# Eight fixed expert weight slots, filled during Wo and the norm, and token stores issued first, in a two-layer decoder step

## What is computed

```python
for layer in range(DEPTH):                       # DEPTH = 2
    if layer < DEPTH_A:                          # layer 0: RWKV-7 time mix
        h, sh, s_fin, v_first = rwkv7_time_mix(x, ...)
    else:                                        # layer 1: dilated window attention
        h = dilated_mixture_attention(x, kv_ext, ...)
    x = layer_norm(ALPHA * x + h, ...)
    m = hier_moe(x, ...)                         # 16 experts, 2 chosen for each token
    x = layer_norm(ALPHA * x + m, ...)
    if layer == DEPTH_A - 1:
        kv_new = einsum('btd,dgsnh->btgsnh', x, p['b_w_kv'])
```

## Time and profile before

| | |
|---|---|
| runs, us | 1735.44, 1732.94, 1730.12; median 1732.94 |
| span of the profiled execution | 1731.9 us (its time from outside is not given; the median of the runs is 1.0 us above the span) |
| busy: TensorE matmul, DVE, ACT, GpSimd | 1557.1, 574.7, 365.6, 196.4 us |
| moved by DMA | 331.28 MB, mean 191 GB/s |
| phases, layer 0 | Wo and norm 482 to 553 us, routing 553 to 578, experts 578 to 861 |
| phases, layer 1 | Wo and norm 1295 to 1366 us, routing 1366 to 1391, experts 1391 to 1673, spill 1675 to 1694 |

### The profile page before, as it was taken

One profiled execution on the slowest core, in us unless ns is written; L12 is line 12 of the kernel. 1 busy time (PEld: TensorE's weight loads), 2 busy tenths in 40 slices (PEclk: granted clock), 3 DMA queues, 4 the chain that ended last, 5 costly groups with the idle time before them and its releaser, 6 DMA issues. The chain is left out here.

```text
span 1731.9 us, 46273 instructions
## 1 busy us (share of the span) xinstructions
PE 1557.1 (90%) x20468; PEld 1156.1 (67%) x20468; DVE 574.7 (33%) x1499; ACT 365.6 (21%) x913; POOL 196.4 (11%) x190
## 2 busy tenths in 40 slices
PE   7999999996897699999859899999999689999980
PEld 6878868875676465555548788887878555555550
DVE  5121445664454321212163100005655521211115
ACT  1023334331501010101131001115650101111113
POOL 1000014643400300000020000000000030000002
PEclk8999999999889799999969999999999789999995
DMA  9410001000523999999971185552120699999994
GB/s 297 164 32 25 1 3 36 29 29 28 181 73 140 339 375 381 383 383 381 373 209 63 64 143 118 126 112 81 44 69 7 229 327 383 380 387 375 385 342 154
DMA packets 218228, 331.28 MB, mean 191 GB/s; under 512 B 70488, under 2 KB 117376, under 8 KB 218032
## 3 DMA queue, kind: packets, MB, share of 16 engines
q1 hardware_dynamic: 193648, 285.33, 48.3%
q0 software_dynamic: 8208, 25.57, 5.5%
q10 hardware_dynamic: 16176, 17.43, 2.9%
HBM read 295.93 MB, written 32.39 MB: 190 GB/s over the span
## 5 line engine op out<-in xcount | busy, mean ns | idle before, releaser
L1979 PE MATMUL bank<-ring_extra,xT 128*32 128x256 f32 x3264 | 181.1, 379 | 0.0
L2443 PE MATMUL bank<-x_early,ring 128*128 128x256 f32 (+1 forms) x768 | 173.5, 387 | 5.7 <-PEq L198 3.9
L1979 PE MATMUL bank<-ring,xT 128*32 128x256 f32 x2880 | 167.3, 388 | 3.2 <-issue 1.6
L2443 PEld LDWEIGHTS bank<-x_early,ring 128*128 128x128 f32 x768 | 146.6, 192 | 28.8 <-issue 4.4
L1979 PEld LDWEIGHTS bank<-ring_extra,xT 128*32 128x32 f32 x3264 | 107.4, 110 | 67.3 <-issue 2.7
L1979 PEld LDWEIGHTS bank<-ring,xT 128*32 128x32 f32 x2880 | 97.6, 112 | 67.1 <-issue 11.6
L1653 DVE TENSOR_TENSOR sg<-sg,bank 128x128 f32<-128x128 f32 x96 | 27.0, 281 | 304.3 <-ACT sg L1832 304.3
L1997 PE MATMUL bank<-ring_extra,hT 128*32 128x256 f32 x1920 | 107.7, 380 | 2.6 <-DVE hT L1661 1.8
L1832 ACT ACTIVATE sg<-bank 128x128 f32<-128x128 f32 x96 | 26.6, 277 | 363.6 <-PE bank L1979 363.6
L376 PE MATMUL bank<-mix,ring 128*128 128x260 f32 x448 | 100.5, 384 | 0.0
L376 PEld LDWEIGHTS bank<-mix,ring 128*128 128x128 f32 x448 | 84.5, 190 | 15.3 <-ACT k L558 2.4
(11 more groups left out here) (416 smaller groups left out, 2309.1 us busy)
## 6 DMA issues: line engine op xcount, KB each, us to landing
ring_extra<-in_moe_w_down SPq DMA_DIRECT2D x40, 1024.0 KB
ring_extra<-in_moe_w_gate SPq DMA_DIRECT2D x70, 512.0 KB, 10.1
ring_extra<-in_moe_w_up SPq DMA_DIRECT2D x70, 512.0 KB, 13.6
ring<-in_moe_w_gate SPq DMA_DIRECT2D x62, 512.0 KB, 6.8
ring<-in_moe_w_up SPq DMA_DIRECT2D x62, 512.0 KB, 13.7
ring<-in_moe_w_down SPq DMA_DIRECT2D x26, 1024.0 KB, 17.4
ring<-in_a_w_rkv SPq DMA_DIRECT2D x12, 1024.0 KB
expert_out<-yo ACTq DMA_DIRECT2D x128, 96.0 KB, 6.4
```

Source lines behind the costliest of these rows:

```text
L1979: ins = pe.matmul(ps[u][32 * q:32 * q + 32, 0:256], xT[:, kt, 32 * u:32 * u + 32], gate_up(w, kt % 2, q), start=kt == 0, stop=kt == KT - 1)
L2443: ins = pe.matmul(ps[2 * (job % 3) + h][:, 0:n], w[:, kt_, rr, :], z[:, kt_, lo:lo + n], start=kt_ == 0, stop=kt_ == 7)
```

## The change

`add_slots` places the eight extra slots at fixed addresses, one call per layer, before `output_norm`. In layer 0 five of them (`dead`) lie where tiles of the time mix are no longer used once its gate is done, and three (`later`) overlap what `output_norm` still reads; in layer 1 all eight lie at the top of the SBUF. `output_norm` gets the range of slots that it may fill, `early_slots`. SP's stream there becomes: load all slots free at the phase's start, store the tokens, then wait for and load the four Wo slots. In `expert_layer` two fences keep the phase's tiles off the slots, a few tiles change places, and the pair gathers and the key/value rows use the six oldest slots (`v_ring`) instead of fixed ones.

```diff
+    def add_slots(self, layer, offsets):
+
+        more = [self.nc.alloc_sbuf_tensor_at(f"ring_extra{layer}{i}", [128, SLOT], F32, offset=at) for i, at in enumerate(offsets)]
+        self.slots = self.slots[0:RING] + [t[:, :] for t in more]
...
-def output_norm(core, z, rows, layer, feed, stop, final_rows, x):
+def output_norm(core, z, rows, layer, feed, stop, final_rows, x, early_slots):
...
             @block.sync
             def _(sp):
-                feed.upto(sp, 4, stop)
+                feed.upto(sp, 0, stop, early_slots)
                 for i, t in enumerate(order):
                     sp.wait_ge(final, i + 1)
                     sp.dma_start(core.tokens[128 * t:128 * t + tile_rows(t), :], final_rows[0:tile_rows(t), t, :]).then_inc(core.tokens_stored, 16)
+                feed.upto(sp, 4, stop, early_slots)
...
-        extra = core.sb(own, "ring_extra", [128, EXTRA, SLOT])
-        core.slots = core.slots[0:RING] + [extra[:, i] for i in range(EXTRA)]
         every = range(RING + EXTRA)
...
-        pair = [extra[:, i].rearrange("p (k d) -> p k d", k=2) for i in range(TILES)]
-        keys_values = [extra[:, i - 1 if i else TILES][:, 0:1536] for i in range(TILES)]
...
         v_ring = [core.slots[s] for s in v_slots]
+        pair = [v_ring[i].rearrange("p (k d) -> p k d", k=2) for i in range(TILES)]
+        keys_values = [v_ring[i - 1 if i else TILES][:, 0:1536] for i in range(TILES)]
...
-                output_norm(core, f["w"], rows, 0, feed, MOE0_END, home, early)
+                rows_end = low + 4 * KT * ROWS + 4 * TILES * D
+                dead = [rows_end + 4 * SLOT * i for i in range(3)] + [low + 5 * 4 * KT * ROWS + 4 * SLOT * i for i in range(2)]
+                later = [low + 4 * 4 * KT * ROWS + 4 * SLOT * i for i in range(2)] + [low + 6 * 4 * KT * ROWS]
+                core.add_slots(0, dead + later)
+                output_norm(core, f["w"], rows, 0, feed, MOE0_END, home, early, range(RING + len(dead)))
...
-            output_norm(core, x, rows, 1, feed, MOE1_END, rows, x)
+            top = SBUF_TOP - 4 * SLOT * EXTRA
+            core.add_slots(1, [top + 4 * SLOT * i for i in range(EXTRA)])
+            output_norm(core, x, rows, 1, feed, MOE1_END, rows, x, range(RING + EXTRA))
```

More of the change, by code:

```diff
@@ L1470, in gate_up, with expert_layer @@
     return slot.rearrange("p (m k n) -> p m k n", m=2, k=2)[:, :, i, 128 * q:128 * q + 128]
-def expert_layer(core, rows, x, layer, stores, feed, stop, next_stop, kv=None):
+def expert_layer(core, rows, x, layer, stores, feed, stop, next_stop, kv=None, fences=None):
     nc, ps, io = core.nc, core.banks, core.io
     with ExitStack() as own:
+        if fences:
+            core.sb(own, "low_fence", [128, fences[0]])
+        v_x = core.sb(own, "spill_x", [128, D])
+        L = core.sb(own, "logits", [128, TILES, 20])
+        g = core.sb(own, "g", [128, TILES, 4, 3])
+        if fences:
+            core.sb(own, "high_fence", [128, fences[1]])
         plan = {"slots": core.sb(own, "slots", [128, 2, TILES], I32), "weights": core.sb(own, "weights", [128, 2, TILES]),
                 "expert": core.sb(own, "expert", [128, SPILLS], I32), "spills": core.sb(own, "spills", [128, 1], I32)}
-        extra = core.sb(own, "ring_extra", [128, EXTRA, SLOT])
-        core.slots = core.slots[0:RING] + [extra[:, i] for i in range(EXTRA)]
         every = range(RING + EXTRA)
         wr, br = core.router[:, layer], core.router_bias[:, layer]
-        L = core.sb(own, "logits", [128, TILES, 20])
-        g = core.sb(own, "g", [128, TILES, 4, 3])
         s = core.sb(own, "s", [128, TILES, 8])
@@ L1509, in expert_layer @@
         yo = [core.sb(own, f"yo{i}", [128, SUBS, 256]) for i in range(2)]
-        v_x, v_y = core.sb(own, "spill_x", [128, D]), core.sb(own, "spill_y", [128, 2, 256])
+        v_y = core.sb(own, "spill_y", [128, 2, 256])
         picks = v_x[:, 0:2 * TILES * CAP].rearrange("p (u t c) -> p u t c", u=2, t=TILES)
@@ L2165, in _ @@
                                                 in_offset=bass.IndirectOffsetOnAxis(ap=plan["slots"][0:n, k, t:t + 1], axis=0)).then_inc(gat[i][k], 16)
-        core.slots = core.slots[0:RING]
 class BiasTables:
@@ L2680, in program @@
             rows = home
-            expert_layer(core, rows, x, 0, to_table, feed, MOE0_END, KV_END, (kF, v0))
+            small = D + 20 * TILES + 12 * TILES
+            fences = (3 * SLOT, (later[-1] + 4 * SLOT - rows_end) // 4 - 3 * SLOT - small)
+            expert_layer(core, rows, x, 0, to_table, feed, MOE0_END, KV_END, (kF, v0), fences)
+            assert nc.sbuf_base <= SBUF_TOP
             core.next_phase()
```

## The result

| | before | changed |
|---|---|---|
| median of 13 runs each, us | 1734.84 (1730.12 to 1736.44) | 1739.25 (1734.62 to 1743.02) |
| ratio, 95% interval | | 1.0032 (1.0023 to 1.0041) |
| profiled execution: time, span | -, 1731.9 | 1736.27, 1734.0 |
| granted clock, mean | 0.953 | 0.953 |

The forecast was 1730.4 us, range 1726.0 to 1735.5. The change is **slower by 0.3%**: a move of +4.4 us where -2.5 was forecast. Part of the miss in the absolute number is the offset: time and span of a run lie 2.3 us apart, not 1.0 (1736.27 against 1734.0), so the sum should have been made against 1734.2.

A forecast was written before the change was run, and what follows sets the result against it. TensorE, 90% busy, was taken to wait on the first gather, not weights. Gather -5.6, barrier +3.6, steady state -0.5 gave -2.5 us from 1732.94, the median of three runs: 1730.4 us, range 1726 to 1735.5.

The forecast's parts named there:

- What bounds the kernel: Whole kernel: TensorE 90% busy, waiting on the first gather, not weights; a quiet DMA queue there is the possible gain.
- Part 1: During Wo: early loads of 7.3 and 8.4 MB fit inside its 64 us and cost nothing.
- Part 2: First gather of each layer: finds an empty queue, saving 2.85 and 2.71 us, 5.6 us together.
- the second rival: First gather: queues already take turns, so only 1 us saved per layer; 1734.0 us, chance 0.15.
- Part 3: Barrier between norm and expert layer: SP arrives 1.35 and 2.2 us later, costing 3.6 us.
- Part 4: GpSimd's scatters, list load and third expert's gather: start 1.35 and 2.2 us later, just in time; nothing in the sum.
- Part 5: Steady state after the first expert: remaining load lead may pull the spill's list forward, saving 0.5 us, bounds 0 and 2.7.
- SP's late loads go into a full queue: Before the two barriers: 14 loads take 1.3 us each instead of 0.5; 1741.6 us, chance 0.03.
- Expert 0 at full clock: First expert: shorter stand-still leaves the clock up, saving 8 us in two layers; 1722.4 us, chance 0.08.

The follow-up runs named there:

- r3: Kernel before with the token stores moved ahead of the four loads, no early slots: 1741.53 us, ratio 1.0048.
- r9: Kernel before, unchanged, run again on the third chip: 1734.05 us, ratio 1.0010.
- r13: Kernel before with five id scatters in place of ten, leaving work out: 1730.81 us, ratio 0.9990.
- r2: Changed kernel with the four Wo slots filled behind the barrier, chunks going to other slots: 1750.85 us, ratio 1.0091.
- r7: Changed kernel with the four Wo slots filled behind the barrier, each chunk in its same slot: 1727.34 us, ratio 0.9984.
- r11: Same kernel as r7 (four loads behind the barrier) on another chip: 1732.71 us, ratio 0.9999.
- r15: Kernel of r7 (four loads behind the barrier) with five id scatters instead of ten: 1725.77 us, ratio 0.9965.
- r6: Changed kernel with six unread matmuls ahead of expert 0's transposes, to warm the clock: 1728.68 us, ratio 0.9995.
- r12: Changed kernel with both the four loads behind the barrier and the six clock-warming matmuls: 1734.80 us, ratio 1.0017.
- r4: Changed kernel with the ten id scatters held until expert 0's gate/up matmuls are done: 1763.27 us, ratio 1.0163.
- r17: Changed kernel, unaltered, run again on the fifth chip: 1739.96 us, ratio 1.0038.
- r18: Changed kernel with five id scatters instead of ten, on the same chip as r17: 1728.03 us, ratio 0.9974.
- r14: Changed kernel with five id scatters instead of ten, on the fourth chip: 1726.83 us, ratio 0.9979.
- r5: Changed kernel with the ten id scatters issued once more into a table nothing reads: 1754.88 us, ratio 1.0146.
- r8: Changed kernel with expert 1's gather issued behind the ten id scatters, so these start sooner: 1741.08 us, ratio 1.0068.
- r16: Kernel of r5 (scatters doubled) again, on the fourth chip: 1755.52 us, ratio 1.0138.

## Why the prediction was wrong

**What bounds the kernel: half right.** That no matmul waits for a weight, and that the gather and the barrier are what the change touches, held. I took expert 0's duration for a constant. The row that gave it away was there: 15.9 us of idle by "issue" in 59 places before L1979, and 10.9 of them lie in the two stretches of expert 0. I used it only to say that no DMA stands behind it. After, it is 27.2 us in 73, 22.5 of them in expert 0:

```profile
  issue: 27.2, 73
```

**Part 1, the early loads: right.** Seven and eight chunks moved during Wo, which ended at 545.7 us as before.

**Part 2, the gather: right in size, wrong in worth.** 4.37 and 4.51 us instead of 7.26 and 7.12: -5.5 us, forecast -5.6. Over the runs a first gather takes 4.1 to 4.6 us with SP's queue quiet and 7.0 to 7.4 with loads in it (both layers of r3, r9 and r13, layer 0 of r2, r7, r11 and r15). The Trainium skill, "DMA: Bandwidth & Descriptors", section "Queues, rings and completion order", has each DMA engine take turns between its queues, a whole packet at a time. The 1 us that the second rival made of it, by half of the bandwidth for each queue, is not borne out: it was 2.9 and 2.6 us. Whether turns of whole packets would give these, no run shows. But on the chips with steps the 5.5 us are given back in expert 0, 2.3 + 3.0 us.

**Part 3, the barrier: mechanism right, size off.** Forecast +1.35 and +2.2, measured +1.73 and +3.02, +4.75 instead of +3.6. The six and eight loads took 3.5 and 5.0 us, 0.6 us each instead of 0.50. SP in layer 1, from the end of its stores:

```profile
1363.33 0.43 SPq L227 DMA_DIRECT2D ring<-in_moe_w_gate  x1
1363.81 0.84 SPq L227 DMA_DIRECT2D ring<-in_moe_w_up  x1
...
1367.82 0.55 SPq L227 DMA_DIRECT2D ring<-in_moe_w_up  x1
```

The eight that I measured by had Wo's silence before them, these had five stores of tokens; that the stores make the difference is likely and not shown.

**Part 4, "what runs behind", is the step that failed.** It said of the scatters "1.35 and 2.2 us later, while TensorE starts earlier ... Nothing in the sum". I asked only whether expert 2's gather would still be in time (it was, with room: issued at 591.23 instead of 598.00). I did not ask what TensorE does while the scatters run. On a chip with steps expert 0 ends 10.3 us after the tenth scatter is issued (10.9 and 9.9 before, 10.3 and 10.2 changed; 12 to 13 where the clock falls), so the scatters' shift, 2.1 and 2.7 us, is the change's cost, and the gather's gain is none of it.

**Part 5: not shown.** 0.9 us less behind layer 1's expert 0, forecast 0.5; but the same stretch takes 324.5 and 325.8 us in the two profiles of the kernel before and 323.2 to 326.4 in the four of the changed one, so agreement here is luck.

**The rivals.** "SP's late loads go into a full queue" had the right side and a time near the truth (1741.6) by a mechanism that is not there: its loads would have taken 1.3 us each. Expert 0 at full clock did not come; r6 and r12 made it so, and with steps it gained nothing (r12). All rivals shared the forecast's blind spot: each changed the beginning of expert 0, none its length.

**What the sum would have been** with the right terms: +1.7 + 3.0 (barrier) + 0.5 (routing to gather, layer 0) - 5.5 (gather) + 5.3 (expert 0) = +5.0, beside 4.4 in the medians.

No version clearly beats the kernel before on every chip. The four loads behind the barrier (r7, r11) make the early slots harmless or better, 0.998 and 1.000, and 0.997 of the change on the same chip (1732.71 / 1738.25). Five scatters less in each layer took 11.9 us off the changed kernel on a chip with steps, more than anything else tried, but those kernels leave work out, and on the fourth chip they took 1.0 us off the kernel before.

## What to carry to other kernels

When a change moves the start of a stretch, check what sets its end before booking the gain: look at every engine that is busy across the stretch, also those that nobody waits for. Idle time by "issue" inside a dense matmul group is a finding, to be laid beside the other engines' timelines. Issue DMAs behind a barrier rather than ahead of it when nothing before the barrier needs them, and when moving them keep each chunk in its slot, or a fixed reader elsewhere pays (r2: 22.7 us).

## What the runs showed of the hardware

- **Ten small indirect scatters (up to 128 rows of 4 bytes, one in 1.28 us) hold TensorE back**: after 108 to 134 of its instructions (143 once) it starts them singly or in bursts of up to nine, 0.70 us from one to the next, until 2 to 3 us after the last scatter is issued. Moving them moves it (r4), halving them ends it (r17, r18). Beside the 12.6 to 12.7 us of r13 it costs 1.6 to 2.9 us in the kernel before, and beside the 12.7 to 13.4 of r14 and r18 it costs 4.3 to 5.3 in the changed one (6 to 7 where the clock falls).
- It is not there always: all kernels with ten scatters on three chips had it, as had the first pair of profiles, and none with ten or more on two others (r5 to r8, r16), r7 and r11 being the same kernel. Whether that is the chip stays open, and so does how the scatters reach TensorE. A supply of instructions that runs low fits the count and the bursts. The Trainium skill, "Runtime: NRT & Kernel Launch", section "Instruction fetch mechanics", has instructions fetched ahead in blocks of 256 by a DMA queue of the engine's own and calls the cost mostly hidden. The trace has one such 16 KB packet in 580 to 588 us of the changed kernel, ahead of the steps; but r7, without steps, has one in 576 to 584 us, just where its expert 0 begins as well, that took no longer (0.96 us both), so nothing here shows that it is the cause. Untried: scatters of fewer rows, and another queue for them.
- A gather of 96 rows took 4.1 to 4.6 us from issue to use with SP's queue quiet and 7.0 to 7.4 with weight loads in it; issued behind ten scatters and beside loads it took 8.75 us (r8).
